# A transformer block kernel in fp32: its first three convolution units made by plain fp32 matmuls from an input normalised tile by tile, with c spread by TensorE and the squares of x on two engines

## The reference

```python
mod = silu(c) @ mod_w + mod_b                         # c: one row of 1024
sh1, sc1, g1, sh2, sc2, g2 = split(mod, 6)
h = rms_norm(x, norm1_g) * (1.0 + sc1) + sh1
proj = h @ w_in                                       # 1024 -> cv_a, cv_g, hg_q, hg_f, ..., 7680 columns
u = cv_a * sigmoid(cv_g)                              # 512 channels
u = causal_conv(u, w, width=31) + b                   # one filter per channel
y_conv = silu(layer_norm(u)) @ w_proj
```

## Time and profile before

| | us |
|---|---|
| median of 3 runs (lowest, highest) | 3539.19 (3539.17, 3542.03) |
| the profiled execution's own time | 3537.95 |
| its span | 3536.2 |
| PE busy | 3437.2 (97%) |
| POOL busy | 1787.4 (51%) |
| DVE busy | 1623.3 (46%) |
| ACT busy | 1311.9 (37%) |

### The profile page before, as it was taken

One profiled execution on the slowest core, in us unless ns is written; L12 is line 12 of the kernel. 1 busy time (PEld: TensorE's weight loads), 2 busy tenths in 40 slices (PEclk: granted clock), 3 DMA queues, 4 the chain that ended last, 5 costly groups with the idle time before them and its releaser, 6 DMA issues.

```text
span 3536.2 us, 46926 instructions
## 1 busy us (share of the span) xinstructions
PE 3437.2 (97%) x15480; PEld 2785.8 (79%) x15480; DVE 1623.3 (46%) x2482; ACT 1311.9 (37%) x1802; POOL 1787.4 (51%) x2327
## 2 busy tenths in 40 slices
PE   5988999999999999999999999999999999999999
PEld 4877776788888888788877888888887887878887
DVE  6867576444454436712323433543458223233443
ACT  3344555322232224734543222322237445532221
POOL 4533444555555555554355555555555443455554
PEclk9999999999999999999999999999999999999999
DMA  5211253322222222222123222222222222222222
GB/s 197 96 54 54 91 178 116 118 95 95 98 92 101 96 95 89 78 96 78 60 84 108 96 95 95 95 99 97 95 92 81 90 80 70 72 90 102 95 96 106
DMA packets 90983, 336.94 MB, mean 95 GB/s; under 512 B 10096, under 2 KB 10480, under 8 KB 90224
## 3 DMA queue, kind: packets, MB, share of 16 engines
q1 hardware_dynamic: 85392, 313.68, 25.5%
q10 hardware_dynamic: 5472, 21.65, 1.8%
HBM read 333.19 MB, written 2.10 MB: 95 GB/s over the span
## 4 chain that ended last, share of the span: by engine, by line
PE 86%; DVE 4%; DVEq 4%; ACT 3%; issue 2%; POOL 0%; ACTq 0%; POOLq 0%
PE ps L435 25%; PE ps L436 25%; PE ps L437 25%; DVEq L1693 1%; PE ps L524 1%; PE ps L568 1%; PE ps L569 1%; PE ps L570 1%; PE ps L841 1%; PE ps L821 1%; PE ps L628 1%; DVE arena L2036 1%; PE ps L696 1%; DVEq L2038 1%; PE ps L832 0%
## 5 line engine op out<-in xcount | busy, mean ns | idle before, releaser
L426 POOL TENSOR_TENSOR w_lo<-raw,w_hi 128x256 fp32r<-128x256 f32 x2280 | 1777.1, 810 | 1727.4 <-ACT w_hi L922 1727.2
L922 ACT ACTIVATE w_hi<-raw 128x1024 fp32r<-128x1024 f32 x572 | 602.2, 1055 | 1067.4 <-PE ps L437 1042.3
L435 PE MATMUL ps<-a_hi,w_lo 128*128 128x512 f32 x2256 | 896.2, 397 | 32.4 <-POOL w_lo L426 21.5
L437 PE MATMUL ps<-a_hi,w_hi 128*128 128x512 f32 x2256 | 881.0, 391 | 0.0
L436 PE MATMUL ps<-a_lo,w_hi 128*128 128x512 f32 x2256 | 880.2, 390 | 0.0
L435 PE MATMUL ps<-b_hi,w_lo 128*128 128x512 f32 x2112 | 830.4, 393 | 8.0 <-DVE b_lo L1629 4.0
L436 PE MATMUL ps<-b_lo,w_hi 128*128 128x512 f32 x2112 | 824.7, 390 | 0.0
L437 PE MATMUL ps<-b_hi,w_hi 128*128 128x512 f32 x2112 | 824.5, 390 | 0.0
L435 PEld LDWEIGHTS ps<-a_hi,w_lo 128*128 128x128 f32 x2256 | 424.7, 188 | 127.7 <-POOL w_lo L426 23.3
L437 PEld LDWEIGHTS ps<-a_hi,w_hi 128*128 128x128 f32 x2256 | 424.2, 188 | 90.4
L436 PEld LDWEIGHTS ps<-a_lo,w_hi 128*128 128x128 f32 x2256 | 424.9, 188 | 86.6 <-issue 3.1
(11 more groups left out here) (246 smaller groups left out, 2721.2 us busy)
## 6 DMA issues: line engine op xcount, KB each, us to landing
raw<-in_stream SPq DMA_DIRECT2D x573, 512.0 KB, 3.2
arena<-in_mod_w ACTq DMA_DIRECT2D x32, 512.0 KB, 4.2
arena<-in_mod_w SPq DMA_DIRECT2D x16, 512.0 KB, 8.1
xres<-in_x_t SPq DMA_DIRECT2D x1, 2048.0 KB, 7.5
xres<-in_x_t ACTq DMA_DIRECT2D x1, 2048.0 KB, 7.5
arena<-in_lru ACTq DMA_DIRECT2D x2, 1024.0 KB, 6.8
out_t<-xres SPq DMA_DIRECT2D x1, 2048.0 KB, 6.3
arena<-in_c_row SPq DMA_DIRECT2D x1, 512.0 KB, 8.9
```

Of the source, the lines that this page charges most:

```text
L426: last = pool.tensor_tensor(w_lo[:, s, part], raw[:, s, part], w_hi[:, s, part].bitcast(F32), ALU.subtract)
L435: pe.matmul(out, lo, x_hi, start=start, stop=False)
L437: return pe.matmul(out, hi, x_hi, start=False, stop=stop)
L922: act.activation(w_hi[:, slot, :], raw[:, slot, :], ACT.Copy).then_inc(hi_ready, 1)
```

## The change

Three units (value 0, gate 0 and value 1 of the convolution) leave the ring. Their weights come as plain fp32 in `first_w`, and TensorE makes them with one fp32 matmul for each k tile from the input itself, not from a pair. UNITS goes from 570 to 567, and the ring begins with gate 1.

The input is made in place in `xres`, a tile at a time, in three steps on three engines: POOL multiplies by `rt` (`x_scaled`), ScalarE applies scale and shift (`first_ready`) and rounds to `a_hi`, and VectorE subtracts for `a_lo` after all columns. x is reloaded later in both kernels. The columns come in pairs (scale k, shift k), and ScalarE adds their constants.

c is loaded as one row, and TensorE spreads it over the partitions with two matmuls against ones into PSUM, where silu is applied in place. x comes in four DMAs. ScalarE squares the even tiles, VectorE the odd ones, and TensorE sums all eight. `consts_ready` is signalled after `ones`, `cols` and two columns; the rest of the constants stands behind it, and the last masks behind POOL's eight multiplications; `masks_ready` tells VectorE of their end.

```diff
 sp:
-            sp.dma_start(xres[:, :, :], x_t).then_inc(x_loaded, 16)
-            sp.dma_start(c_act, c_row.to_broadcast([P, D])).then_inc(c_loaded, 16)
-            for u in range(MOD_FIRST):
...
-            for s in range(RING):
-                sp.dma_start(raw[:, s, :], stream[s]).then_inc(raw_loaded[s], 16)
+            sp.dma_start(c_line, c_row).then_inc(c_loaded, 16)
+            for i in range(4):
+                sp.dma_start(xres[:, 2 * i:2 * i + 2, :], x_t[:, 2 * i:2 * i + 2, :]).then_inc(x_part_loaded[i], 16)
+            for n in range(MOD_FIRST):
+                load_mod(n)
+                if n == 3:
+                    for i in range(FIRST):
+                        sp.dma_start(first_w[:, i, :], first[i]).then_inc(first_loaded, 16)
+                if n in (11, 13, 15):
+                    load_raw((n - 11) // 2)
 pool:
+            pool.wait_ge(first_rt, 1)
+            for k in range(KT):
+                pool.tensor_tensor(xres[:, k, :], xres[:, k, :], rt, ALU.mult).then_inc(x_scaled, 1)
 pe:
-            x_stats()
+            pe.wait_ge(c_loaded, 16)
+            for i in range(2):
+                last = pe.matmul(ps[:, 5 + i, :], ones[0:1, 0:P], c_line[:, i * S:i * S + S], start=True, stop=True)
+            last.then_inc(c_spread, 1)
+            for k in range(KT):
+                pe.wait_ge(odd_squares if k % 2 else even_squares, k // 2 + 1)
+                last = pe.matmul(ps[:, 7, :], ones_p, first_sq[:, k, :], start=k == 0, stop=k == KT - 1)
+            last.then_inc(first_summed, 1)
+            def project_first(*banks):
+                pe.wait_ge(first_loaded, 16 * FIRST)
+                for k in range(KT):
+                    pe.wait_ge(first_ready, k + 1)
+                    last = [pe.matmul(ps[:, bank, :], first_w[:, i, k * P:k * P + P], xres[:, k, :], start=k == 0, stop=k == KT - 1)
+                            for i, bank in enumerate(banks)]
...
-            project_fresh(bank_v(), bank_a())
-            for j in range(1, CT):
+            project_first(bank_v(), bank_a(), bank_v())
+            project_fresh(bank_a())
+            for j in range(2, CT):
 act:
-            for k in range(KT):
-                x_square(k)
-            inverse_rms(D)
-            for u in range(LEAD):
-                round_unit(u, 16)
-            act.wait_ge(mod_ready, 1)
-            round_tiles(a_hi, range(KT), modp[:, 0:KT])
+            first_square(0)
+            act.wait_ge(c_spread, 1)
+            act.activation(c_act, c_act, ACT.Silu).then_inc(c_ready, 1)
+            for k in range(2, KT, 2):
+                first_square(k)
...
+            for k in range(KT):
+                act.wait_ge(mod_used, 2 * k + 2)
+                act.activation(scale1[:, k:k + 1], modp[:, KT + k:KT + k + 1], ACT.Identity, scale=par(PAR1, "norm1_g", k), bias=first_bias[:, k:k + 1])
+                act.activation(first_shift[:, k:k + 1], modp[:, k:k + 1], ACT.Identity, bias=par(PAR1, "mod_b", k))
+                act.drain()
+                act.wait_ge(x_scaled, k + 1)
+                act.activation(xres[:, k, :], xres[:, k, :], ACT.Identity, scale=scale1[:, k:k + 1], bias=first_shift[:, k:k + 1]
+                               ).then_inc(first_ready, 1)
+                act.drain()
+                act.activation(a_hi[:, k, :], xres[:, k, :], ACT.Copy).then_inc(op_rounded, 1)
+                if k >= KT - LEAD:
+                    round_unit(k + LEAD - KT, 16)
 dve:
+            for k in range(1, KT, 2):
+                dve.wait_ge(x_part_loaded[k // 2], 16)
+                dve.tensor_tensor(first_sq[:, k, :], xres[:, k, :], xres[:, k, :], ALU.mult).then_inc(odd_squares, 1)
+            dve.wait_ge(c_ready, 1)
+            for n in range(MOD_FIRST):
+                unit, u = mod_stage[:, n % MOD_RING, :], n // 2 if n % 2 else KT + n // 2
+                dve.wait_ge(mod_loaded[n % MOD_RING], 16 * (n // MOD_RING + 1))
+                dve.scalar_tensor_tensor(unit, unit, 1.0, c_act, ALU.mult, ALU.mult, accum_out=modp[:, u:u + 1]).then_inc(mod_used, 1)
+            for k in range(KT):
+                low_part(a_lo[:, k, :], a_hi[:, k, :], xres[:, k, :]).then_inc(op_ready, 1)
...
-            take_rt()
-            norm(a_hi, a_lo, scale1, modp[:, 0:KT])
```

More of the change, by code:

```diff
@@ L180, in need, with build @@
         eng.wait_ge(sem, value)
-def build(nc, x_t, c_row, par1, par2, lru, mod_w, stream, out_t):
+def build(nc, x_t, c_row, par1, par2, lru, mod_w, first, stream, out_t):
     with ExitStack() as ctx:
@@ L319, in build @@
         c_loaded, par_loaded, x_loaded, lru_loaded, out_stored = sem("c_loaded"), sem("par_loaded"), sem("x_loaded"), sem("lru_loaded"), sem("out_stored")
+        x_part_loaded = [sem(f"x_part_loaded{i}") for i in range(4)]
+        first_loaded, masks_ready, c_spread = sem("first_loaded"), sem("masks_ready"), sem("c_spread")
+        even_squares, odd_squares, first_summed, first_rt, x_scaled, first_ready = (
+            sem("even_squares"), sem("odd_squares"), sem("first_summed"), sem("first_rt"), sem("x_scaled"), sem("first_ready"))
         mod_loaded = [sem(f"mod_loaded{i}") for i in range(MOD_RING)]
@@ L377, in _ @@
             pool.memset(ones[:, :], 1.0)
+            pool.memset(cols[:, :], 0.0)
+            pool.drain()
+            pool.memset(eps_col, EPS)
+            pool.memset(one_col, 1.0)
+            pool.drain()
+            pool.memset(cols[:, 127:128], 0.0).then_inc(consts_ready, 1)
             pool.memset(neg_tri_made, -1.0)
@@ L418, in _ @@
             pool.drain()
-            pool.memset(cols[:, 127:128], 0.0).then_inc(consts_ready, 1)
+            pool.memset(cols[:, 127:128], 0.0).then_inc(masks_ready, 1)
             with pool.Fori(0, UNITS // RING) as i:
@@ L577, in _ @@
             pe.wait_ge(consts_ready, 1)
-            x_stats()
+            pe.wait_ge(c_loaded, 16)
[12 more added lines that the diff above has]
+                            for i, bank in enumerate(banks)]
+                for made in last:
+                    tile(made)
             def conv_mean():
@@ L992, in x_square, with first_square @@
                     c.sq.n += 2
-            act.wait_ge(consts_ready, 1)
-            act.wait_ge(par_loaded, 16)
-            act.wait_ge(c_loaded, 16)
+            act.preload_act_table_set("silu_and_others")
+            def first_square(k):
+                act.wait_ge(x_part_loaded[k // 2], 16)
+                act.activation(first_sq[:, k, :], xres[:, k, :], ACT.Square).then_inc(even_squares, 1)
+            first_square(0)
+            act.wait_ge(c_spread, 1)
             act.activation(c_act, c_act, ACT.Silu).then_inc(c_ready, 1)
+            for k in range(2, KT, 2):
+                first_square(k)
             logs()
@@ L1646, in _ @@
             dve.tensor_scalar(keep, keep, -1.0, 1.0, ALU.mult, ALU.add)
-            for k in range(KT):
[L1649 to L1655, removed]
             def mod_columns(first, end, at, scale, g):
                 dve.drain()
-                ins = dve.tensor_tensor(modp[:, first:end], modp[:, first:end], par(PAR1, "mod_b", first, end - first), ALU.add)
-                if first == 0:
-                    ins.then_inc(mod_ready, 1)
+                dve.tensor_tensor(modp[:, first:end], modp[:, first:end], par(PAR1, "mod_b", first, end - first), ALU.add)
                 dve.drain()
                 dve.scalar_tensor_tensor(scale, modp[:, at * KT:(at + 1) * KT], 1.0, par(PAR1, g, 0, KT), ALU.add, ALU.mult)
-            mod_columns(0, MOD_FIRST, 1, scale1, "norm1_g")
+            dve.wait_ge(masks_ready, 1)
             dve.tensor_scalar(q_col, par(PAR1, "sbq_g"), SB_DH ** -0.5, None, ALU.mult)
@@ L1937, in _ @@
             gated_split(xres, sb_gate)
-            dve.wait_ge(x_loaded, 32)
+            dve.wait_ge(x_loaded, 16)
             def add_tile(m, scale):
@@ L2333 @@
         "mod_w": np.ascontiguousarray(a["mod_w"][0].T.reshape(MODS, P, D)),
+        "first": np.ascontiguousarray(np.stack(early)),
         "stream": np.ascontiguousarray(np.stack(order)),
```

40 lines of the change are left out of this document (28 added, 12 removed).

## The result

The changed kernel took 3518.57 us (median of 4 runs, 3515.09 to 3520.38) against 3539.18 for the kernel before (3538.74 to 3542.03): a ratio of 0.9939, interval 0.9922 to 0.9956. It is 20.6 us faster where 23 were forecast, inside the range of 3511 to 3523. Its profiled execution took 3517.43 for a span of 3515.7, so 20.5 us less span than before.

A forecast was written before the change was run, and what follows sets the result against it. VectorE's convolution chain, hung on the end of the fourth unit, was taken as the bound. Its start at 48.0 against 71.61 gave 23.6 us, shaved to 23: 3537.95 - 23 = 3515 (3516.2 against the median), range 3511 to 3523.

The forecast's parts named there:

- Rival D: After the convolution: gain made but not carried, TensorE's later work depending on something unmoved; half given back, 3527.7; chance 0.03.
- Sum of squares at 14.2: TensorE's eight fp32 matmuls summing the squares, from 7.1 at 0.86 us each (6.9 us), end at 14.2.
- the spread fills 3.7 us, so I take full stride: Spreading c keeps TensorE busy 3.7 us, so the sums behind it run at 0.86 us a matmul, not 1.83.
- rival A: TensorE's whole first burst at the slow level, sums done at 21.7: 16.9 us gained, 3522.3; chance 0.12.
- First input at 18.0: First fp32 input ready at 18.0: 1/rms row at 15.7, POOL's first tile at 17.1, ScalarE's scale and shift 0.72.
- Slow start of the units, 1.8: A break of nearly 4 us before TensorE's three fp32 units probably costs a slow start, 1.8 us (half of 3.6).
- Columns done at 36.2: VectorE's last column done at 36.2, DMA setting the pace: last pair lands at 35.0 with 403 GB/s.
- rival B: Columns slower (queue at 383 GB/s, 1.7 us late, or VectorE held beside POOL): 20.5 us gained, 3518.7; chance 0.09.
- a_lo at 44.2: VectorE's eight subtractions for a_lo from 36.2, about six beside POOL at 1.07 us, the rest alone, end at 44.2.
- Rival E: VectorE's a_lo and POOL's low parts alternate whole instructions, a_lo done at 47.3: 20.5 us gained, 3518.7; chance 0.04.
- The convolution at 48.0: VectorE's convolution starts at 48.0, 23.6 us earlier than 71.61, VectorE's own queue last; TensorE alone would allow 47.2.
- Rival C: Slower than before: fp32 matmuls stay at 1.83 us throughout, convolution starts 6.3 us later, 3545.5; chance 0.02.

The follow-up runs named there:

- full_height: The changed kernel with c spread by matmuls as high as the array (128x128 ones, c's row in a zeroed tile): 3518.73 us, ratio 0.9944 to the kernel before.
- fill: The changed kernel with four more fp32 matmuls of ones into an unused bank between the sum of squares and the first input: 3515.28 us, ratio 0.9941.
- split_units: The changed kernel's new front without the fp32 units; the first three units come from the ring as pairs again: 3533.09 us, ratio 0.9986 to the kernel before.
- again: The changed kernel once more, with no edit: 3518.63 us, ratio 0.9946 to the kernel before.
- c_in_sbuf: The changed kernel, but silu writes c to SBUF, where the columns read it: 3526.98 us, ratio 0.997 to the kernel before.
- setup: The changed kernel with VectorE's small keep arithmetic and most set-up moved from behind a_lo into its wait among the columns: 3516.11 us, ratio 0.9939.

## Why the prediction was right, and where it was off

What bounded the kernel: right. VectorE's convolution chain, hung on the fourth unit, carried the gain to the end whole (20.1 us at the mean, 20.5 in the span). Rival D fell. The convolution was forecast at 48.0 and started at 51.4; the terms follow, first those of TensorE's side, then those of VectorE's.

Sum of squares at 14.2 (the terms as written, 7.1 + 6.9, give 14.0): it ended at 16.6. The step "the spread fills 3.7 us, so I take full stride" failed. The spread's matmuls are one row deep, and the level was still low behind them: of the sums' sixteen weight loads the first eight are slow, so four of the eight sums ran at 1.71 us and four at 0.86. A part of rival A came true: half of the sums were slow, where A had all of them. In full_height the fast level came 1 to 6 us sooner, but in two of its three profiles still behind the start of the first sum, so full stride from there would have been early even at full height. The Trainium skill, "TensorE: Matmul & The Clock Gate", Part 1, has it that activity releases the slow level. The traces agree: in fill, where matmuls of ones fill all but 0.4 of the 3.8 us of idle time, no slow record is left in the units.

First input at 18.0: 20.25, the 2.4 us of the sums; POOL's tile was cheaper (1.23 for 1.4), ScalarE dearer (0.81 for 0.72).

Slow start of the units, 1.8: 2.9, slow from 20.4 to 26.3. It is a term of the same kind, mis-sized: I took the 3.6 us of one start in the trace, and such stretches at the start of the units lasted 2.8 us (split_units) to 5.9 us (again). fill removed it. With 20.6 us for the 24 matmuls, right, the units ended at 44.1 instead of 40.4. TensorE's side would by this have let the convolution start at 50.9 instead of 47.2.

Columns done at 36.2: 37.8. The queue moved 380 GB/s over 2 to 20 us and 404 over 20 to 37, where I had 403 all through; the 1.7 us of delay that rival B gives for a slower queue came, as 1.6. Since VectorE was the last, these count in full at the convolution; TensorE did not wait for a column. That POOL's multiplication is free beside columns that read c from PSUM was right, and c_in_sbuf gives the other place its price: 7.4 us at the convolution.

a_lo at 44.2: 46.5, of which 1.6 are the columns; 1.08 a piece, but for all eight and not for six, as POOL made low parts beside nearly all of them: 0.7 more. Rival E fell for a_lo: not 1.39 a piece. For the longer columns (1.15 + 1.23 alone against 2.21 together) turns were nearly whole. The small work behind a_lo cost 3.6 instead of 2.5, because a part of it ran beside POOL: an operation on 128x4 took 0.45 there and 0.16 in setup, where POOL was idle:

```profile
15.96 0.16 DVE L1719 TENSOR_TENSOR cols<-cols 128x4 f32<-128x4 f32 x1
```

The convolution at 48.0: 51.4. VectorE's own misses, 1.6 + 0.7 + 1.1, are these 3.4 us; TensorE's, 3.7 us, lay beside them and cost next to nothing, as fill shows (0.2 us). That VectorE would be the last, by 0.8, came out with 0.5, but by luck: both sides were late by nearly the same, and where the slow stretches fell shorter (setup) TensorE's side was 1.5 us earlier. Rivals B and E both gave a time of 3518.7, 0.1 us from what was measured; neither is its cause as written, since E did not happen and of B only the 1.6 us of the queue did (its 2.7 us for the eighth input stands on no row). Rival C: the fp32 matmuls of the units stood 0.86 apart from 26.3 us on, as at the earlier trace rows. What I held against C, full stride right after a wait of 1.76, is not sure to hold: behind the wait of 2.19 at the mean in the changed kernel the same matmuls took 5.37 us in place of 3.67.

## What to carry to other kernels

When a start is a relay over five engines, write the landmarks of the new relay down on each engine to the last hand-over; of two engines that end within a microsecond of each other, speeding up the one that is first moves nothing (fill). Two halves of a change can be worth less apart than together (3.7 and 10.4 us against 20.2 by the landmarks here, with the reserve made above), so trying one half and dropping it can mislead. A value that VectorE multiplies by beside a busy POOL belongs in PSUM, and a plain fp32 matmul (0.86 against 0.68 us for three fp32r) is cheap where it does away with the splitting that TensorE would wait for.

## What the runs showed that I had not expected

Behind matmuls one row deep the fast level came later (at 9.9 to 12.7 us in eight profiles) than behind the same ones at full height (at 6.8 to 9.0 in three). The slow stretch at the start of the units differed between executions by up to 3 us (from 20.1 to 23.4 in setup, from 20.4 to 26.3 in the changed kernel), which moves the units' end by more than a microsecond. POOL's affine selects, which read int8 masks of 64 columns, went from 0.32 to 1.05 us each beside VectorE's work with two inputs in SBUF. Why a_lo and the low parts overlap more than the columns and the multiplications do stays open.
